# Hybrid decoder block: order of the merge-gate loads, places of the small transposes, first feed-forward group, and tile offsets

## The reference

```
h  = RMSNorm(x);  p = h @ w_in
A  = gated DeltaNet(q, k, v, z, alpha, beta)      # 8 heads of 128
B  = forgetting attention(q, k, v, f, out gate)   # 16 heads of 64
y  = sigmoid(gA) * (A @ w_branch_a) + sigmoid(gB) * (B @ w_branch_b)
x  = x + y @ w_out
x  = x + (silu(h2 @ w_gate) * (h2 @ w_up)) @ w_down,   h2 = RMSNorm(x)
out = RMSNorm_final(x)
```

## Time and profile before

| | us |
|---|---|
| median of 3 runs | 1360.84 (1360.41 to 1361.93) |
| the profiled execution's own time | 1359.85 |
| its span in the profile | 1358.1 |
| PE busy | 1278.7 (94%) |
| PEld (weight loads) busy | 1063.9 (78%) |
| DVE, ACT, POOL busy | 506.1, 473.8, 465.9 |
| mean granted TensorE clock | 0.971 of full |

### The profile page before, as it was taken

The page is one execution under the profiler, slowest core; times in us unless marked ns, Lnnn a source line. Parts: engine busy times, 40 slices in busy tenths (PEclk is TensorE's granted clock), DMA queues, the critical chain, the costliest instruction groups (busy, mean ns, idle before and its releaser), DMA issues.

```text
span 1358.1 us, 18270 instructions
## 1 busy us (share of the span) xinstructions
PE 1278.7 (94%) x6573; PEld 1063.9 (78%) x6573; DVE 506.1 (37%) x897; ACT 473.8 (35%) x889; POOL 465.9 (34%) x226
## 2 busy tenths in 40 slices
PE   5999979989899899999999998879989999999997
PEld 4868869889788798888888877667768888888886
DVE  4334452342343421566666663341123333331001
ACT  5344462523533423444444431211322222321122
POOL 5334440321411403322222223332234444443443
PEclk9989989998998989999999998989999999999999
DMA  5323320211211203332222215341223333332221
GB/s 165 85 68 93 96 75 24 71 47 36 83 48 43 75 24 103 103 89 85 85 85 85 85 47 186 108 121 50 78 70 101 93 93 97 104 108 81 99 99 62
DMA packets 169638, 113.69 MB, mean 84 GB/s; under 512 B 6257, under 2 KB 157922, under 8 KB 169586
## 3 DMA queue, kind: packets, MB, share of 16 engines
q1 hardware_dynamic: 163218, 98.26, 24.8%
q10 hardware_dynamic: 6368, 14.72, 3.0%
HBM read 104.54 MB, written 8.42 MB: 83 GB/s over the span
## 4 chain that ended last, share of the span: by engine, by line
PE 34%; issue 21%; POOL 7%; DVE 2%; ACT 2%; DMA 0%; POOLq 0%; DVEq 0%; SPq 0%; ACTq 0%
PE ps L1192 21%; PE ps L1550 9%; POOL w_lo L506 7%; PE ps L1280 2%; PE ps L1174 1%; ACT w_hi L569 1%; PE ps L1487 1%; DMA gin<-gate_dram 0%; ACT gin L781 0%; DVE h_lo L846 0%; ACT h_hi L787 0%; DVE x2T L835 0%; DVE Tm L963 0%; DVE tmp L1107 0%; DVE y_hi L835 0%
## 5 line engine op out<-in xcount | busy, mean ns | idle before, releaser
L506 POOL TENSOR_TENSOR w_lo<-raw,w_hi 128x1024 fp32r<-128x1024 f32 x170 | 418.6, 2463 | 826.4 <-ACT w_hi L569 826.4
L1192 PE MATMUL ps<-h_hi,w_lo 128*128 128x512 f32 x992 | 408.6, 412 | 0.0
L1192 PE MATMUL ps<-h_hi,w_hi 128*128 128x512 f32 x992 | 392.0, 395 | 9.3 <-POOL w_lo L506 6.0
L1192 PE MATMUL ps<-h_lo,w_hi 128*128 128x512 f32 x992 | 393.0, 396 | 0.0
L569 ACT ACTIVATE w_hi<-raw 128x1024 fp32r<-128x1024 f32 x170 | 179.8, 1060 | 562.2 <-PE ps L1192 466.4
L1192 PEld LDWEIGHTS ps<-h_hi,w_hi 128*128 128x128 f32 x992 | 188.3, 190 | 42.1 <-POOL w_lo L506 7.0
L1192 PEld LDWEIGHTS ps<-h_lo,w_hi 128*128 128x128 f32 x992 | 187.4, 189 | 39.2 <-issue 1.0
L1192 PEld LDWEIGHTS ps<-h_hi,w_lo 128*128 128x128 f32 x992 | 189.5, 191 | 31.9 <-issue 1.2
L884 DVE SCALAR_TENSOR_TENSOR tmp<-ps,prm,tmp 128x511 f32<-128x511 f32 (+2 forms) x72 | 53.9, 748 | 93.8 <-ACT tmp L599 88.7
L1130 DVE TENSOR_TENSOR f_lo<-tmp,f_hi 128x512 f32 (+1 forms) x22 | 39.5, 1794 | 33.8 <-ACT f_hi L801 33.8
L1280 PEld LDWEIGHTS ps<-Yn,Tm 128*128 128x128 f32 (+1 forms) x384 | 49.2, 202 | 3.2 <-ACT Yn L685 1.5
(11 more groups left out here) (233 smaller groups left out, 1686.2 us busy)
## 6 DMA issues: line engine op xcount, KB each, us to landing
raw<-in_w_in SPq DMA_DIRECT2D x80, 512.0 KB, 3.8
raw<-in_w_gate SPq DMA_DIRECT2D x22, 512.0 KB, 3.7
raw<-in_w_up SPq DMA_DIRECT2D x22, 512.0 KB, 3.7
raw<-in_w_down SPq DMA_DIRECT2D x22, 512.0 KB, 3.2
gate_dram<-gate ACTq DMA_DIRECT2D x24, 256.0 KB, 2.0
cumb<-cum_dram ACTq DMA_DIRECT2D x8, 512.0 KB, 3.4
raw<-in_w_branch_a SPq DMA_DIRECT2D x8, 512.0 KB, 3.7
raw<-in_w_branch_b SPq DMA_DIRECT2D x8, 512.0 KB, 3.6
```

Of the source, the lines that this page charges most:

```text
L506: pool.tensor_tensor(w_lo[:, r % 2, :], raw[:, r, :], w_hi[:, r % 2, :], ALU.subtract)\
L1192: return pe.matmul(ps[:, bank, :], wts[wl][k], acts[xl][:, k, :], start=(n == 0), stop=(n == len(PASSES) - 1))
```

## The change

It alters five things and no arithmetic.

- SP: in the loop load_gates(i) stands ahead of load_ab(i+1), and load_gates(3) ahead of load_out(0).
- PE, w_out stage: x2_turn(j-1) ahead of n = 19, the residual ahead of n = 22.
- First feed-forward group: x2_turn(7) in unit 0 ahead of n = 16, wide_row in unit 1 ahead of n = 20; on POOL the power stands between the subtractions for units 1 and 2.
- `wfin`, the final norm's weights on all partitions, has no tile of its own but uses tmp, and its 512 KB load stands on SP's queue behind 20 of the 22 w_down loads and waits for the last f_lo.
- Three stages get 13 * LINE floats (1,664 bytes) of padding in front, the attention stage's four LINE tiles go behind b_lo, and wfin's 4 KB disappear.

```diff
+            pad_fox = sb("pad_fox", [P, 13 * LINE])
             vT = sb("vT", [P, T])
...
-            scratch = sb("scratch", [P, LINE])
-            nmax = sb("nmax", [P, LINE])
-            psum_p = sb("psum_p", [P, LINE])
-            rsum = sb("rsum", [P, LINE])
             o_nat = sb("o_nat", [P, TT, P])
...
             b_lo = sb("b_lo", [P, KT, T], F32R)
+            scratch = sb("scratch", [P, LINE])
+            nmax = sb("nmax", [P, LINE])
+            psum_p = sb("psum_p", [P, LINE])
+            rsum = sb("rsum", [P, LINE])
...
+            pad_out = sb("pad_out", [P, 13 * LINE])
             y_hi = sb("y_hi", [P, KT, T], F32R)
...
+            pad_ffn = sb("pad_ffn", [P, 13 * LINE])
             f_hi = sb("f_hi", [P, FT, T], F32R)
             f_lo = sb("f_lo", [P, FT, T], F32R)
-            wfin = sb("wfin", [P, D])
...
+        wfin = tmp[:, :, :].rearrange("p a n -> p (a n)")
...
             with sp.Fori(1, KT // 2 - 1) as i:
+                load_gates(i)
                 load_ab(i + 1)
-                load_gates(i)
+            load_gates(KT // 2 - 1)
             load_out(0)
-            load_gates(KT // 2 - 1)
             load_out(1)
...
-            sp.wait_ge(unit_done, 4 * OUT0 + 1)
-            sp.dma_start(wfin[:, :], norm_final_w.partition_broadcast(P)).then_inc(wfin_loaded, 16)
...
+            sp.wait_ge(ffn_low, led(ffn_low, FT))
+            sp.dma_start(wfin, norm_final_w.partition_broadcast(P)).then_inc(wfin_loaded, 16)
...
-            for r in range(3):
+            for r in range(2):
                 low_part(FFN0, r)
             pool.wait_ge(ms_ready, TT + 1)
             power(rstd[:, 0:TT], ms[:, 0:TT], TT).then_inc(rstd_ready, 1)
-            low_part(FFN0, 3)
+            for r in range(2, 4):
+                low_part(FFN0, r)
...
-            def unit(q, r, hi, lo, tasks=(), last_input=None):
+            def unit(q, r, hi, lo, tasks=(), last_input=None, at=None):
...
-                    if tasks and n % every == every - 1:
+                    if tasks and (n in at if at else n % every == every - 1):
...
-                     None if j else (y_low, led(y_low, KT)))
+                     None if j else (y_low, led(y_low, KT)), (19, 22) if j else (22,))
...
-                    tasks = ([x2_turn(KT - 1)], [], [wide_row], [])[r] if first else ()
-                    unit(i + FFN0, r, h_hi, h_lo, tasks, (h_low, 2 * KT) if first and r == 0 else None)
+                    tasks = ([x2_turn(KT - 1)], [wide_row], [], [])[r] if first else ()
+                    unit(i + FFN0, r, h_hi, h_lo, tasks, (h_low, 2 * KT) if first and r == 0 else None,
+                         (20,) if r else (16,))
```

More of the change, by code:

```diff
@@ L1166, in _ @@
                         out=x_res[:, t - 1, :], in0=ps[:, 2 * t - 2:2 * t, :].rearrange("p b n -> p (b n)"),
-                        scalar=rstd[:, t - 1:t], in1=wfin[:, :], op0=ALU.mult, op1=ALU.mult)\
+                        scalar=rstd[:, t - 1:t], in1=wfin, op0=ALU.mult, op1=ALU.mult)\
                         .then_inc(fin_ready, 1)
```

## The result

The changed kernel took 1314.55 us (median of 4 executions, 1314.02 to 1318.75), against 1360.62 for the kernel before beside it: a ratio of 0.9674, 95% interval 0.9658 to 0.9691. The profiled execution took 1314.04 us, its span is 1312.3. Against the one before that is 45.8 us, where the sum said 40.1. Executions of one and the same kernel turned out to spread more than I had said: ten of the changed one lie between 1314.0 and 1320.9, median 1316.5. Two of the twelve executions of r_before (1451 and 1972 us, mean granted clock 0.84 and 0.60) are slow ones, and no ratio here counts them.

A forecast was written before the change was run, and what follows sets the result against it. PE, busy 94% of the span, bounds the kernel, so time is won at its pauses and in shorter steps. 20.7 + 6.8 + 7.3 + 5.3 = 40.1 us takes 1359.85 to 1319.8, median 1320.7; range 1316.5 to 1327.

The forecast's parts named there:

- Gate loads: Branch stage: gates issued ahead of the weight loads remove PE's pauses at three turns, 20.7 us; chance of no effect 0.04.
- two middle turns: Branch stage, group 1 to 2 and group 2 to 3: pauses of 5.4 us each, both gone.
- turn to w_out: From the last branch group to w_out: pause of 10.3 us, 9.9 gone and 0.4 left, between 0 and 1.
- x2_turn and residual: w_out stage: transposes moved 8 matmuls on start after what they wait for, all 6.8 us gone; moving the residual is free.
- First feed-forward group: Its start: of 8.1 us of pauses 7.3 gone, 0.55 left at wide_row; late wide row as rival, chance 0.06.
- the 0.2 that unit 3 was to wait: First feed-forward group: unit 3's w_lo ready at 18.1, wanted at 17.9, so PE waits 0.2 us.
- wfin: w_down stage: its late 512 KB load costs 0, with over 30 us of cover.
- Offsets: Branch, w_out and w_down: tiles at multiples of 2048 bring steps to 0.2267 us, 5.3 us; chance of no effect 0.14.
- the rule that the prediction set against this term: Trainium skill page: independent SBUF read ports for moving and stationary operands, PE never waits; offsets worth 0, time 1326.0.
- the median lies 1.0 above it: 1320.7: Whole kernel: forecast profiled execution 1319.8 us, the median of executions 1.0 above that.
- 0.6 (y_low): Turn to w_out: PE's wait for y_low is at most 0.6 us in the changed profile.
- 0.1 (unit 5): w_out stage: if the transposes in unit 5 miss, 0.1 us of the 6.8 comes back.

The follow-up runs named there:

- r_before: The kernel before, unchanged, profiled and timed again: 1359.5 us, ratio 0.9992 to the kernel before.
- e2: Kernel before with only SP's order changed, gate loads ahead of the next group's weight loads: 1337.1 us, ratio 0.9838.
- e3: Kernel before with only x2_turn ahead of n = 19 and the residual ahead of n = 22 in the w_out stage: 1351.3 us, one time.
- e5_no_offsets: Changed kernel without the padding and the moved lines, all reorderings and late wfin load kept: 1322.95 us, ratio 0.9756 to the kernel before.

## Why the prediction was right, and where it was wrong

- **Gate loads.** Right. The two middle turns are gone in full, the turn to w_out leaves 0.26 us (forecast 0.4). e2 alone: 21.0 against 20.7.
- **x2_turn and residual.** Right: no wait for x2T or the squares, 6.9 against 6.8 (e3).
- **First feed-forward group.** Right in mechanism and size: 7.3 against 7.3. wide_row starts 0.55 late behind the blocked diagonal; the 0.2 that unit 3 was to wait isn't there.
- **wfin.** Nothing, as forecast; no stretch of w_down is longer.
- **Offsets.** Right in mechanism: moving the tiles alone turns 0.2324 into 0.2267. Size 6.0 instead of 5.3: branch stage 2.3, w_down 2.8, w_out 0.6 instead of 0.45, attention 0.2 where I took 0 within a bound of 2.0. By the rule that the prediction set against this term the offsets were worth 0 and the time 1326.0; the measurement decides.
- **The step that failed** is the one that wasn't a term of the sum: "the median lies 1.0 above it: 1320.7", with the range built from the edits' bounds and "the three runs lie within 1.5 us". I took the time of the unchanged part as fixed, so its change stood at nothing in the sum. It was worth 5.1 of the 45.8 us, and the clock did it: 553.0 us ahead of the first vT transpose in the profile on which the sum rests, 547.9 in the changed one, and 547.9, 548.8 and 554.7 in three profiles of the changed kernel. Falls of the clock that differ come beside a pause of 2.3 us in the convolution and, without one, in DeltaNet's small matmuls. By their times (only the first has a profile), three of the four executions that made the result had a short part ahead. The sum is right for what it summed, 40.1 against 40.7, but a little of that agreement is luck: over four profiles of the kernel before, the part behind lay between 803.6 and 805.1, so 40.7 could have been 39.2.
- **What a typical execution gains.** The median is 1359.0 over 54 executions of the kernel before, all on record but the two named above, and 1316.5 over ten of the changed one: 42.5 us, nearer to the sum than the result's 46.1. The 1316.5 lies only at the very edge of the range.
- **The range.** Its upper end doesn't follow from the bounds given: they add 0.6 (y_low), 0.1 (unit 5) and 1.3 us (first feed-forward group), which makes 1322.7 and not 1323.5. Nothing hangs on it here, as the miss is below.
- **How it could be seen.** The granted clock over the first 547 us of the profile before is 0.96, so about 22 us of that part are clock (an estimate: 0.04 x 547), and a single profile shows one outcome of it. A range must allow for some of them to fall the other way, by the spread seen here about 3 to 4 us to each side.

## What to carry to other kernels

Price a stall from the last matmul ahead to the first at full pace, and treat the clock part as a chance, in the stretches that the change doesn't touch too, and there also where PE doesn't pause. Compare two kernels on the stretch behind a common event: three profiles of the changed kernel agreed there to 0.1 us, four of the kernel before, with its five pauses of over 3 us, to 1.5. Look at the steps between matmuls of the same shape in every stage: when they differ, look at the start bytes of the two operands. And where a load is late, ask what stands ahead of it in its queue: two issues exchanged in SP's order were worth half of this gain.

## What the hardware showed that I hadn't expected

- A 128x512 fp32r matmul whose moving and stationary tiles start a multiple of 256 bytes apart steps by 0.2267 us, at 128 or 384 over it by 0.2324 to 0.2334, at the same granted clock of 1.00. 0, 256 and 512 over were fast; smaller differences than 128 weren't tried, and what in the chip does it isn't known. By the Trainium skill, "TensorE: Matmul & The Clock Gate", Step-by-step, a weight load takes no bandwidth from the running matmul. As a rule on time that doesn't hold here, since the place of one operand against the other costs 0.006 us a step; whether the ports are the reason isn't shown.
- The clock doesn't follow from the length of a pause alone: 3.34 us of idle time cost none in e5_no_offsets, 3.33 us in e2_gates cost 12 matmuls at 1.2 GHz. Nor does it take a pause: at 412 us in the kernel before it fell while PE had no wait, and 16 matmuls of 128x128 took 3.51 us instead of 1.95.
